# Gate rows loaded from GpSimd's queue, two subtractions given to GpSimd, and other orders in the first norm, three attention pairs, the gates and the norm stages of a transformer kernel

## The reference, cut to what matters

```python
mod = silu(c) @ ada_w[i] + ada_b[i]
sh_a, sc_a, g_a, sh_f, sc_f, g_f = split(mod, 6)
h = rms_norm(x, norm_g[i, 0]) * (1 + sc_a) + sh_a
y = moba_attention(h, ...) if i % 2 == 0 else diff_attention(h, ...)
x = x + g_a * rms_norm(y, norm_g[i, 1])
h = rms_norm(x, norm_g[i, 2]) * (1 + sc_f) + sh_f
x = x + g_f * rms_norm(swiglu(h, ffn_w_in[i], ffn_w_out[i]), norm_g[i, 3])
```

## Time and profile before

| | us |
|---|---|
| median of 3 runs | 1014.02 (1012.82 to 1015.51) |
| the profiled execution | 1013.14 |
| its span, first to last instruction | 1011.3 |
| busy: PE / DVE / ACT / POOL | 919.6 / 682.3 / 484.7 / 36.3 |
| mean granted TensorE clock | 0.968 of full speed |

### The profile page before, as it was taken

The page is one execution under the profiler, slowest core; times in us unless marked ns, Lnnn a source line. Parts: engine busy times, 40 slices in busy tenths (PEclk is TensorE's granted clock), DMA queues, the critical chain, the costliest instruction groups (busy, mean ns, idle before and its releaser), DMA issues.

```text
span 1011.3 us, 14324 instructions
## 1 busy us (share of the span) xinstructions
PE 919.6 (91%) x6067; PEld 842.1 (83%) x6071; DVE 682.3 (67%) x775; ACT 484.7 (48%) x631; POOL 36.3 (4%) x92
## 2 busy tenths in 40 slices
PE   0599998999999699899889999998898999999995
PEld 0599986989999688799769999997887899999974
DVE  5989865878777667766677655455796655545465
ACT  2354546444443355677465334344483534443463
POOL 2111000101100000000000000000000000000000
PEclk9699999999999899899999999999899899999998
DMA  8999871899887942345339756673334456565511
GB/s 339 358 348 321 294 218 40 297 338 374 302 291 256 318 159 85 125 138 196 130 134 316 252 172 203 211 237 125 125 126 166 158 176 200 176 203 205 205 53 42
DMA packets 127810, 212.75 MB, mean 210 GB/s; under 512 B 4753, under 2 KB 98050, under 8 KB 127746
## 3 DMA queue, kind: packets, MB, share of 16 engines
q1 hardware_dynamic: 116562, 168.82, 49.2%
q0 software_dynamic: 11184, 43.01, 11.7%
HBM read 210.75 MB, written 1.06 MB: 209 GB/s over the span
## 4 chain that ended last, share of the span: by engine, by line
PE 76%; DVE 11%; ACT 5%; issue 3%; DMA 3%; SPq 0%; DVEq 0%; ACTq 0%
PE ps L566 24%; PE ps L568 23%; PE ps L567 23%; DVE w_lo L1382 3%; DVE ada_sum L1400 3%; ACT w_hi L1003 2%; DMA ada_raw<-in_ada_w 1%; DVE h_lo L1482 1%; PE ps L782 1%; DMA raw<-in_ffn_w_in 1%; DMA raw<-in_moba_w_qkv 1%; ACT yg L1045 1%; PE ps L655 1%; ACT h_hi L1039 1%; DVE yg L1477 1%
## 5 line engine op out<-in xcount | busy, mean ns | idle before, releaser
L1382 DVE TENSOR_TENSOR w_lo<-raw,w_hi 128x2048 fp32r<-128x2048 f32 x145 | 331.6, 2289 | 184.3 <-ACT w_hi L1003 184.1
L1003 ACT ACTIVATE w_hi<-raw 128x2048 fp32r<-128x2048 f32 x145 | 276.8, 1910 | 244.7 <-PE ps L568 200.7
L566 PE MATMUL ps<-h_hi,w_hi 128*128 128x256 f32 x1216 | 348.4, 287 | 10.3 <-DVE h_lo L1482 8.6
L567 PE MATMUL ps<-h_lo,w_hi 128*128 128x256 f32 x1216 | 346.5, 285 | 0.0
L568 PE MATMUL ps<-h_hi,w_lo 128*128 128x256 f32 x1216 | 346.5, 285 | 0.0
L566 PEld LDWEIGHTS ps<-h_hi,w_hi 128*128 128x128 f32 x1216 | 236.0, 194 | 13.2 <-issue 9.4
L567 PEld LDWEIGHTS ps<-h_lo,w_hi 128*128 128x128 f32 x1216 | 236.1, 194 | 1.2
L568 PEld LDWEIGHTS ps<-h_hi,w_lo 128*128 128x128 f32 x1216 | 235.8, 194 | 0.0
L566 PE MATMUL ps<-w_hi,o_hi 128*128 128x512 f32 x264 | 105.8, 401 | 3.9 <-DVE o_lo L1767 2.2
L567 PE MATMUL ps<-w_lo,o_hi 128*128 128x512 f32 x264 | 103.5, 392 | 0.0
L568 PE MATMUL ps<-w_hi,o_lo 128*128 128x512 f32 x264 | 103.5, 392 | 0.0
(11 more groups left out here) (273 smaller groups left out, 954.0 us busy)
## 6 DMA issues: line engine op xcount, KB each, us to landing
...
```

Source lines behind the costliest of these rows:

```text
L566: T.matmul(out_ap, hi_s, hi_m, start=start, stop=False, skip_group_check=True)
L567: T.matmul(out_ap, hi_s, lo_m, start=False, stop=False, skip_group_check=True)
L1003: A.activation(w_hi[:, n.place], raw[:, n.raw_place], ACT.Copy).then_inc(slab_hi, 1)
L1382: V.tensor_tensor(w_lo[:, n.place], raw[:, n.raw_place], w_hi[:, n.place].bitcast(F32), ALU.subtract).then_inc(slab_lo, 1)
```

## The change

1. `load_gate_rows` moves from SP's queue to POOL's, behind the `ada_w` loads 19, 39, 43 and 47.
2. First norm (z = 0): ACT modulates units 1 and 3 and DVE units 0 and 2 (before, DVE all four), and ACT's `split_hi(1)` comes behind them. In the first pair of layer 0 ACT's `queries_out` comes ahead of `split_hi(3)`.
3. POOL subtracts the lower parts of slab 0 and of slab 20 (`FFN[0] + 4`).
4. `col_slab` with a norm, and `first_two`, multiply `h_hi` by both weight parts first, as soon as `hi_ready` allows, and only then wait for `h_lo`.
5. The gates are split in halves, for b = 0 and 2 into the free `hid_hi`, `hid_lo` and the end of `o_hi`, `o_lo`, inside the last pair (before: behind it, in the output projection's stage).
6. Layer 1, first pair: the 15 small operations of the recurrence (now `decay`) go to chunk 5 of the feed-forward part, the scores come one step earlier, `biased` comes right behind `split_lo(n + 3)`, and one `ada_w` accumulation moves from ahead of `biased` to the pair's end.
7. Output projection: `gate_row` comes ahead of the heads' lower parts; in layer 1 ACT loads the table for the root earlier, and `split_lo(n + 4)` stands ahead of the heads' norm.

```diff
@@ kernel: constants and gate parts
-T_BASE = [0, 4, 6, 8, 10, 14, 18]
+T_BASE = [0, 2, 4, 6, 8, 12, 16]
-        def gate_split(b):
-
-            return [h[:].rearrange("p a b -> p (a b)")[:, 0:D] for h in ((o_hi, o_lo) if b % 2 else (h_hi, h_lo))]
+        def gate_split(b, c):
+
+            if b % 2:
+                return ada_hi[:, c * HALF_D:(c + 1) * HALF_D], ada_lo[:, c * HALF_D:(c + 1) * HALF_D]
+            return [(small, o[:, 6:8])[c].rearrange("p a b -> p (a b)")
+                    for small, o in ((hid_hi[:], o_hi), (hid_lo[:], o_lo))]
@@ SP (load_gate_rows is taken out, with its two calls)
-                load_gate_rows(2 * l)
                 for h in range(2):
                     load_two(Slab(FFN[l] + h), ffn_w_in[l], h, D_FF)
...
-                    if j == FF_CHUNKS - 3:
-                        load_gate_rows(2 * l + 1)
@@ POOL
+            def split_lo(n):
+
+                pool.wait_ge(slab_hi, n.plus(1))
+                if n.first:
+                    pool.wait_ge(slab_lo, n.plus(0))
+                G.tensor_tensor(w_lo[:, n.place], raw[:, n.raw_place], w_hi[:, n.place].bitcast(F32), ALU.subtract)\
+                    .then_inc(slab_lo, 1)
...
+            split_lo(Slab(0))
             pool.wait_ge(ada_acc, 2 * FIRST_MODS)
             pool.dma_start(bias[:], ...)
...
                 load_ada(m)
+                if m == ADA_LATER + 1:
+
+                    split_lo(Slab(FFN[0] + 4))
+                for b, last in enumerate((ADA_LATER - 1, ADA_GA - 1, ADA_GF - 1, len(ADA) - 1)):
+                    if m == last:
+                        load_gate_rows(b)
@@ PE, col_slab (first_two alike)
+                    pe.wait_ge(hi_ready, 4 * z + Z_NEED[z][0])
+                    for o in range(2):
+                        to, cs = ps[:, bank, o * S:(o + 1) * S], slice(o * P, o * P + P)
+                        for k in range(4):
+                            T.matmul(to, wh[:, k, cs], h_hi[:, k], start=k == 0 and o == 0, stop=False,
+                                     skip_group_check=True)
+                            T.matmul(to, wl[:, k, cs], h_hi[:, k], start=False, stop=False, skip_group_check=True)
+                    pe.wait_ge(h_ready, 4 * z + Z_NEED[z][0])
...
+                            T.matmul(to, wh[:, k, cs], h_lo[:, k], start=False, stop=False, skip_group_check=True)
+                    pe.wait_ge(h_ready, 4 * z + Z_NEED[z][1])
@@ PE, first pair of layer 1
-                        v_slab(n + 2, {1: turn_queries_keys, 5: lambda: scores(pairs * 3 + 2)})
+                        v_slab(n + 2, {1: turn_queries_keys, 4: lambda: scores(pairs * 3 + 2)})
@@ ACT, first norm
-            for unit, (t, c) in enumerate(BY_HALF):
-                if unit == 2:
-                    split_hi(Slab(1))
-                hi_part(0, unit, t, c)
+            act.wait_ge(gain_ready, 1)
+            t_modulated(0, 1, 1, 0, gain[:, 0], SH_A)
+            hi_part(0, 0, 0, 0)
+            own_hi_part(1, 1, 0)
+            t_modulated(0, 3, 1, 1, gain[:, 0], SH_A)
+            hi_part(0, 2, 0, 1)
+            own_hi_part(2, 1, 1)
+            split_hi(Slab(1))
@@ ACT, output projection
-                gate_hi(2 * l)
+                if l:
+                    A.preload_act_table(ACT.Sqrt)
                 split_hi(n + 3)
                 copy_turned(pairs, (5, 6))
+                split_hi(n + 4)
                 heads_out(pairs, PAIRS, slice(6, 8))
                 if l:
                     heads_hi(PAIRS, slice(6, 8))
-                split_hi(n + 4)
@@ DVE, first pair of layer 1
+                    if l and first:
+                        split_lo(n + 2)
+                        lambda_sum()
+                        split_lo(n + 3)
+                        biased(pairs + 1, 0)
+                        split_lo(n + 4)
+                        normalised(pairs + 1, 1)
+                        split_lo(n + 5)
+                        ada(ADA_GA + 2)
+                        return
@@ DVE, output projection
-                gate_lo(2 * l)
                 split_lo(n + 3)
+                gate_row(2 * l, (5, 6), (3, 10)[l])
                 if l:
+                    split_lo(n + 4)
                     heads_normalised(PAIRS)
                 heads_low(pairs, slice(6, 8))
-                gate_row(2 * l, (5, 6), (3, 10)[l])
-                split_lo(n + 4)
+                if l == 0:
+                    split_lo(n + 4)
```

More of the change, by code:

```diff
@@ L574, in col_slab @@
                 bank = n.bank if bank is None else bank
-                for k in range(KT):
-                    if z is not None and k % 4 == 0:
-                        pe.wait_ge(h_ready, 4 * z + Z_NEED[z][k // 4])
+                first = 0
+                if z is not None:
+                    first = 4
+                    pe.wait_ge(hi_ready, 4 * z + Z_NEED[z][0])
[6 more added lines that the diff above has]
+                    pe.wait_ge(h_ready, 4 * z + Z_NEED[z][0])
+                    for o in range(2):
+                        to, cs = ps[:, bank, o * S:(o + 1) * S], slice(o * P, o * P + P)
+                        for k in range(4):
+                            T.matmul(to, wh[:, k, cs], h_lo[:, k], start=False, stop=False, skip_group_check=True)
+                    pe.wait_ge(h_ready, 4 * z + Z_NEED[z][1])
+                for k in range(first, KT):
                     for o in range(2):
@@ L1047, in t_modulated, with own_hi_part @@
                 last.then_inc(t_act_ready, 1)
-            def own_hi_part(z, t, c):
-                act.wait_ge(t_act_ready, 2 * (z - 1) + t + 1)
+            def own_hi_part(count, t, c):
+                act.wait_ge(t_act_ready, count)
                 A.activation(h_part(h_hi, t, c), turned_tile(t, c), ACT.Copy).then_inc(hi_ready, 1)
             def gate_hi(b):
-                act.wait_ge(ada_acc, 2 * (ADA_LATER, ADA_GA, ADA_GF, len(ADA))[b])
+                act.wait_ge(ada_acc, 2 * (GATE_PART[b] + 1))
                 if b == 1:
                     act.wait_ge(ada_reduced, 8)
-                else:
-                    act.wait_ge(slab_done, OPROJ[b // 2] + (KT // 2 if b == 3 else 0))
-                A.activation(gate_split(b)[0], ada_sum[:, ADA[(ADA_LATER - 12, ADA_GA - 1, ADA_GF - 1, ADA_GF)[b]][4]],
-                             ACT.Copy).then_inc(gate_hi_ready, 1)
+                elif b == 3:
+                    act.wait_ge(slab_done, OPROJ[1] + KT // 2)
+                for c in range(2):
+                    A.activation(gate_split(b, c)[0], ada_sum[:, ADA[GATE_PART[b]][4], half(c)], ACT.Copy)\
+                        .then_inc(gate_hi_ready, 1)
             def y_squares(b, a, banks, slab, t):
@@ L1177, in pair @@
                         return
-                    split_hi(n + 3)
+                    if not first:
+                        split_hi(n + 3)
                     act.wait_ge(slab_done, n.plus(1))
                     queries_out(ps[:, n.bank])
+                    if first:
+                        split_hi(n + 3)
+                    if j == PAIRS - 1:
+                        gate_hi(2 * l)
                     split_hi(n + 4)
@@ L1687, in pair @@
                         ada(FIRST_MODS + 3 * j + 2)
-                    if l and first:
-                        split_lo(n + 5)
                     normalised(pairs + 1, j + 1)
-                    if l and not first:
+                    if l:
                         heads_low(pairs, heads_before)
-                    if not (l and first):
-                        split_lo(n + 5)
+                    split_lo(n + 5)
                 for j in range(PAIRS):
@@ L1752, in _ @@
                         gate_row(2 * l + 1, (FF_FREE[l], MISC), (9, 11)[l])
+                    if l == 0 and chunk == 1:
+                        dve.wait_ge(slab_lo, n.plus(3))
                     split_lo(n + 3)
@@ L1757, in _ @@
                         ada(ADA_GF + chunk - 1)
+                    elif l and chunk == KT // 2 + 1:
+                        decay()
                     if not last:
```

104 lines of the change are left out of this document (56 added, 48 removed).

## The result

The changed kernel takes 1005.41 us (median of 6 runs, 1001.39 to 1008.24) against 1015.53 us before (median of 6, 1012.82 to 1016.17). The ratio is 0.9908, 95% interval 0.9885 to 0.993, so it is faster by some 9 us, half of the 18.2 that the prediction adds up; the median lies 9.4 above the forecast and just above the upper end of its range. Run again beside the experiments it took 1002.08 us (ratio 0.988, 0.986 to 0.9899).

A forecast was written before the change was run, and what follows sets the result against it. PE, busy 919.6 of 1011.3 us, was taken as the bound, leaving its waits and low clock to gain. Terms summed to 19.9, less 1.7 for a new low stretch: 18.2 gained, 995.8 rounded to 996.0 us, range 990 to 1005.

The forecast's parts named there:

- The gate rows in layer 0: Second gate of layer 0: `ada_w` 40 lands in 6.6 us, spread at 338.85 instead of 345.32, low stretch gone; +8.1 us.
- its first rival: POOL's queue takes SP's place: `ada_w` 40 and 41 land late, gate gives 3.8 instead of 8.1, 1000.3 us; chance 0.15.
- The prediction's own sign for this: Layer 0's second gate: the prediction is wrong if the wait for `ada_w` 40 lasts beyond 336.
- The start: First norm and first pair's keys: first product at 40.7, but slab 4's load decides; 2.0 us lost, bounds 4 lost to 1 gained.
- Upper parts first: PE multiplies upper parts while DVE subtracts the norm's first lower part: +0.7 at norms 1 and 2, +0.6 at norm 4.
- GpSimd's subtraction: Lower parts of slabs 0 and 20: 4 us each, hidden in 6.9 and 6.3 free; rival of a long one, chance 0.07.
- The shared port: Rival at the start: DVE's small SBUF operations and GpSimd's subtraction hold each other up; 0.5 us, 996.5; chance 0.10.
- Layer 1's first pair: Probabilities ready some 7 us ahead, the 5.01 wait and low stretch go, new waits of 0.4 and 2.2; +4.9 us.
- the 1.7 of the sum: Deduction in the sum: one of the new small waits (1.3, 2.2, 1.2) brings a low-clock stretch of its own, −1.7 us.
- Output projection and norm 3: Layer 1: spread's wait 3.21 becomes 1.2, the 2.13 wait and a low stretch go, upper parts first 0.7; +6.9 us.
- The small operations: Layer 1's recurrence operations, 2.9 us, go where DVE sits idle 3.88; were that gone, 2.9 would be paid there.

The follow-up runs named there:

- second profile: The changed kernel run again with no edit, beside the experiments: 1002.08 us, ratio 0.988 to the kernel before; profiled execution 1001.86 us.
- part 1 alone: Kernel before the change with only the gate rows' loads moved to POOL's queue, where the change puts them: 1011.72 us, ratio 0.9971.

## Why the prediction was wrong, point by point

- **The gate rows in layer 0: wrong in size.** "I take 6.6, in the lower half, since SP's loads no longer come in a crowd at that moment: 333.2" is the step that failed. The load took 10.2 us (10.1 and 10.4 in the second profile and with part 1 alone), above the range of the earlier trace rows, and the low stretch stayed, so the term of 8.1 was 2.7 up to the spread; part 1 alone gives 2.9. The row loads ahead of it were counted by their issues of 0.70 and not by the 512 KB that each moves. In the trace they land first, on full DMA engines, but no run shows how much of the 3.6 that the load took longer than assumed is theirs, since the same load took 10.4 with none ahead of it. What is shown is that behind this stop it did not land in time, in nine profiles of nine (the gate waits 4.1 to 5.2), and that issued ahead of the stop it costs the gate nothing and gives the change 4.4 more. The measured 2.7 lies below the prediction's lower bound, 3.8; its first rival had the mechanism, with a chance of 0.15 that was too small. The prediction's own sign for this came: the load is waited for until 346.0, or 337.0 without the 9.0 us by which everything stood later there, beyond its 336.
- **The start: right in sign, wrong in size.** "0.3 for loads issued later" named the right thing and priced it at a tenth. It took slab 4's 8.74 us as a property of the load, though the DMA share of 1.04 says that the stretch is bound by bytes. Then a queue that stands 4.5 us is a hole of 2.8 us which nothing fills, and the whole stage ends that much later: 5.2 with the low stretch of 59.9 to 66.7, for 2.0, and beyond the bound of 4 lost. With the subtraction on VectorE the 3.2 are gone (keys at 58.99). The prediction weighed the subtraction by what PE waits for, and not by what stood behind it on POOL.
- **Upper parts first: right in size, in part by luck.** 0.7 per norm was one lower part. Both units of a norm gain, 1.45, and 0.6 to 0.75 of it goes to a wait for the slab's lower part and to what follows; the prediction names neither in its sum.
- **GpSimd's subtraction:** 4 taken, 4.51 and 4.61 measured. The Trainium skill ("GPSIMD Engine Reference", § 3) has 4497 ns, and the trace agrees. Its place at slab 20 costs nothing.
- **The shared port:** there, with 0.3 us in the change, for the 0.5 of the rival.
- **Layer 1's first pair: right.** The 5.01 went and the new wait is 1.90 for 2.2; in the first profile it brought a low stretch of its own (3.4 us), the 1.7 of the sum, in the second none. The stretch of the table gave 3.6 and 6.0 in the two profiles, for 5.5, which holds the 1.6 of the low stretch behind the gate that did not go.
- **Output projection and norm 3: right.** 2.1 and 4.1 for 2.0 and 4.9; undone one by one, the two waits of 3.28 and 2.13 come back.
- **The small operations** in chunk 5 and the split in the last pair cost nothing to be seen; no run tests them alone.

What stays open is the clock between executions: the same kernel had 45.2 and 31.7 us at 1.2 GHz, and its runs lie between 1001.4 and 1008.2, wider than the error of most terms above. At the start it did not matter: before, PE had 1.2 GHz from 31.1 to 48.2, both profiles of the changed kernel have the full clock there, and among the kernels with slab 0 on VectorE the keys come at 58.99 and 59.07 with a low stretch of 31 to 45 and at 59.03 and 58.73 without. The load decides there, not PE.
